# Dilated attention: first group's logits in two column tiles of 384 keys, value products cut to the rows a key block reaches

## The reference, cut to what matters

```python
off = np.arange(3 * blk)[None, :] - blk - np.arange(blk)[:, None]
band = np.abs(off) <= half            # half = window // (2 * dil) = 64
...
logits = einsum(q, k) * hd ** -0.5 + bias
logits = where(mask, logits, -1e30)
lse = logsumexp(logits);  p = exp(logits - lse);  o = einsum(p, v)
...
wgt = softmax(stack(lses));  o_b = sum(wgt[..., None] * stack(outs))
```

## Time and profile before

| | |
|---|---|
| time, median of 3 runs | 1826.12 us (1824.75 to 1828.1) |
| the profiled execution: time | 1826.74 us |
| its span, first to last instruction | 1825.0 us |
| PE busy | 1765.7 us, 97% |
| DVE, ACT, POOL busy | 801.9, 723.6, 604.0 us |
| mean granted clock of PE, as a share of 2.4 GHz | 0.988 |

### The profile page before, as it was taken

One profiled execution on the slowest core, in us unless ns is written; L12 is line 12 of the kernel. 1 busy time (PEld: TensorE's weight loads), 2 busy tenths in 40 slices (PEclk: granted clock), 3 DMA queues, 4 the chain that ended last, 5 costly groups with the idle time before them and its releaser, 6 DMA issues.

```text
span 1825.0 us, 25256 instructions
## 1 busy us (share of the span) xinstructions
PE 1765.7 (97%) x10862; PEld 1390.1 (76%) x10862; DVE 801.9 (44%) x1342; ACT 723.6 (40%) x1228; POOL 604.0 (33%) x182
## 2 busy tenths in 40 slices
PE   8999999999999999998999999989999999999997
PEld 5778899988888888877888888877684478776456
DVE  8756646623123121114670143145446654526653
ACT  5656665433233332233331222234426533345541
POOL 3534210333333434432454444424332114333112
PEclk9999999999999999998999999989999999999998
DMA  5121200326223323222222232213220012211001
GB/s 205 70 93 24 72 3 25 132 70 191 79 95 104 123 70 110 96 93 69 93 92 93 97 111 93 92 70 140 70 83 10 1 48 97 93 69 47 1 1 47
DMA packets 37504, 144.71 MB, mean 79 GB/s; under 512 B 3155, under 2 KB 15835, under 8 KB 23696
## 3 DMA queue, kind: packets, MB, share of 16 engines
q1 hardware_dynamic: 18944, 121.53, 18.8%
q10 hardware_dynamic: 18448, 21.57, 3.9%
HBM read 140.93 MB, written 5.30 MB: 80 GB/s over the span
## 4 chain that ended last, share of the span: by engine, by line
PE 87%; DVE 5%; ACT 4%; issue 1%; DMA 1%; ACTq 0%; POOL 0%; SPq 0%; POOLq 0%; DVEq 0%
PE bank L407 56%; PE bank L1145 6%; PE bank L613 5%; PE bank L418 4%; PE bank L2196 3%; PE bank L2220 3%; PE bank L2203 2%; DVE WK L978 1%; PE bank L1653 1%; PE bank L1629 1%; PE bank L2149 1%; ACT WK L2330 1%; ACT w_part L365 1%; PE bank L2228 1%; DMA WK<-wgate 1%
## 5 line engine op out<-in xcount | busy, mean ns | idle before, releaser
L407 PE MATMUL bank<-x_part,w_part 128*128 128x512 f32 x3216 | 746.8, 392 | 1.5 <-ACT WK L2309 0.8
L407 PEld LDWEIGHTS bank<-x_part,w_part 128*128 128x128 f32 x3216 | 601.0, 188 | 135.4 <-issue 10.7
L2660 POOL TENSOR_TENSOR w_part<-RAW,w_part 128x2048 fp32r<-128x2048 f32 (+1 forms) x90 | 404.2, 4493 | 678.4 <-ACT w_part L365 678.4
L365 ACT ACTIVATE w_part<-RAW 128x2048 fp32r<-128x2048 f32 (+1 forms) x90 | 165.8, 1842 | 175.5 <-PE bank L407 138.0
L2660 POOL TENSOR_TENSOR w_part<-WK,w_part 128x2048 fp32r<-128x2048 f32 (+1 forms) x30 | 123.7, 4124 | 246.9 <-ACT w_part L365 246.9
L407 PE MATMUL bank<-f_part,w_part 128*128 128x512 f32 x768 | 174.4, 389 | 0.0
L407 PEld LDWEIGHTS bank<-f_part,w_part 128*128 128x128 f32 x768 | 144.1, 188 | 29.9
L1145 PE MATMUL bank<-WK 64*64 64x64 f32 (+1 forms) x1456 | 103.4, 249 | 4.8 <-ACT WK L1311 2.5
L1145 PEld LDWEIGHTS bank<-WK 64*64 64x64 f32 (+1 forms) x1456 | 99.0, 163 | 7.3 <-ACT WK L1311 2.6
L978 DVE SCALAR_TENSOR_TENSOR WK<-bank,COL,WK 128x510 f32<-128x510 f32 (+1 forms) x96 | 71.7, 749 | 48.6 <-ACT WK L920 45.9
L2677 POOL TENSOR_TENSOR WK<-BASE,WK 128x1024 f32<-128x1024 f32 x16 | 30.4, 1898 | 167.5 <-DVE WK L2503 167.5
(11 more groups left out here) (286 smaller groups left out, 2236.1 us busy)
## 6 DMA issues: line engine op xcount, KB each, us to landing
RAW<-wts SPq DMA_DIRECT2D x83, 1024.0 KB, 4.8
WK<-wts SPq DMA_DIRECT2D x23, 1024.0 KB, 4.8
WK<-scratch ACTq DMA_DIRECT2D x16, 256.0 KB, 2.7
WK<-decay_rows ACTq DMA_DIRECT2D x14, 256.0 KB, 6.6
RAW<-wts SPq DMA_DIRECT2D x7, 512.0 KB, 3.5
WK<-wts SPq DMA_DIRECT2D x7, 512.0 KB, 3.4
scratch<-bias_rows ACTq DMA_DIRECT2D x4, 768.0 KB, 8.8
WK<-xT SPq DMA_DIRECT2D x4, 512.0 KB, 7.3
```

Source lines behind the costliest of these rows:

```text
L365: act.eng.activation(high_part(i), raw_part(i), ACT.Copy).then_inc(*act.did(("hi", i)))
L407: mm = pe.eng.matmul(b[:, :], W[w][:, k, c:c + P], src[x][k], start=start and k == 0 and n == 0, stop=stop and k == kn - 1 and n == 2)
L2660: eng.tensor_tensor(low_part(i), raw_part(i), high_part(i).bitcast(F32), ALU.subtract).then_inc(w_split, 1)
```

## The change

In group 0 the 128 queries of residue r are the tokens 4 l + r. The first 64 of them lie in tokens 0 to 255, the last 64 in tokens 256 to 511. With a reach of 64 keys the first half needs only keys 0 to 319 and the second half keys 192 to 511. The changed kernel gives each half 384 keys: 0 to 383 and 128 to 511. The halves are two products with 64 stationary columns each, written to PSUM partitions 0 to 63 and 64 to 127. A row of logits then has 384 + 256 elements in place of 512 + 256.

There are five transposes instead of six. The value product of group 0 becomes six products, three key blocks for each half, each of them only over the queries that the block reaches: widths 48, 48, 16 and 16, 48, 48. The two products of groups 1 and 2 come first, since they write all 128 columns. The bias tile of group 0 comes in two DMAs instead of one.

```diff
+        NEAR = 3 * P
-        LG = wk(31488, 2, 768)      (PT, BI alike)
+        LG = wk(31488, 2, NEAR + 2 * P)
+        REACH = ((0, 48), (16, 64), (48, 64)), ((64, 80), (64, 112), (80, P))
...
-                E.matmul(b[:, :], QB[:, 0, r * P:(r + 1) * P], KB[:, 0, :], start=True, stop=True).then_inc(...)
+                for a in range(2):
+                    mm = E.matmul(b[64 * a:64 * a + 64, 0:NEAR], QB[:, 0, r * P + 64 * a:r * P + 64 * a + 64],
+                                  KB[:, 0, a * P:a * P + NEAR], start=True, stop=True)
+                mm.then_inc(*pe.did(("pe", ("la", n))))
...
-                for k in range(4):
+                for k in range(3):
                     mm = E.transpose(a[:, k * P:(k + 1) * P], LG[:, n % 2, k * P:(k + 1) * P], ident)
...
-                for k in range(6):
-                    v = VB[:, k, 0:P] if k < 4 else VB[:, r, (k - 3) * P:(k - 2) * P]
-                    mm = E.matmul(o[:, 0:P], v, PT[:, n % 2, k * P:(k + 1) * P], start=k == 0, stop=k == 5)
+                for g in (1, 2):
+                    E.matmul(o[:, 0:P], VB[:, r, g * P:(g + 1) * P], PT[:, n % 2, NEAR + (g - 1) * P:NEAR + g * P], start=g == 1, stop=False)
+                for a in range(2):
+                    for k, (lo, hi) in enumerate(REACH[a]):
+                        mm = E.matmul(o[:, lo:hi], VB[:, k + a, 0:P], PT[:, n % 2, k * P + lo:k * P + hi], start=False,
+                                      stop=a == 1 and k == 2)
...
-                A.activation(PT[:, n % 2, 0:512], ps(("ta", n))[:, :], ACT.Copy)...
+                A.activation(PT[:, n % 2, 0:NEAR], ps(("ta", n))[:, 0:NEAR], ACT.Copy)...
...
-                A.dma_start(BI[:, n % 2, 0:512], a).then_inc(bias_in[n % 2], 16)
+                for h in range(2):
+                    a = bass.AP(..., offset=base + 511 - r + h * (64 * (1536 - DIL) + P), ap=[[1536 - DIL, 64], [1, NEAR]])
+                    A.dma_start(BI[64 * h:64 * h + 64, n % 2, 0:NEAR], a).then_inc(bias_in[n % 2], 16)
...
-                V.scalar_tensor_tensor(out=LG[:, n % 2, 0:512], in0=ps(("la", n))[:, :], ..., in1=BI[:, n % 2, 0:512], ...)
+                V.scalar_tensor_tensor(out=LG[:, n % 2, 0:NEAR], in0=ps(("la", n))[:, 0:NEAR], ..., in1=BI[:, n % 2, 0:NEAR], ...)
```

More of the change, by code:

```diff
@@ L1602, in build @@
         VB = wk(29952, TT, 3 * P)
-        LG = wk(31488, 2, 768)
-        PT = wk(33024, 2, 768)
-        BI = wk(34560, 2, 768)
+        NEAR = 3 * P
+        LG = wk(31488, 2, NEAR + 2 * P)
+        PT = wk(33024, 2, NEAR + 2 * P)
+        BI = wk(34560, 2, NEAR + 2 * P)
+        REACH = ((0, 48), (16, 64), (48, 64)), ((64, 80), (64, 112), (80, P))
         BR = wk(12288, 1536)
@@ L1628, in logits @@
                 b = job(("la", n))
-                E.matmul(b[:, :], QB[:, 0, r * P:(r + 1) * P], KB[:, 0, :], start=True, stop=True).then_inc(*pe.did(("pe", ("la", n))))
+                for a in range(2):
+                    mm = E.matmul(b[64 * a:64 * a + 64, 0:NEAR], QB[:, 0, r * P + 64 * a:r * P + 64 * a + 64], KB[:, 0, a * P:a * P + NEAR],
+                                  start=True, stop=True)
+                mm.then_inc(*pe.did(("pe", ("la", n))))
                 b = job(("lb", n))
@@ L1642, in turn @@
                 for k in range(2):
-                    mm = E.transpose(b[:, k * P:(k + 1) * P], LG[:, n % 2, (4 + k) * P:(5 + k) * P], ident)
+                    mm = E.transpose(b[:, k * P:(k + 1) * P], LG[:, n % 2, (3 + k) * P:(4 + k) * P], ident)
                 mm.then_inc(*pe.did(("pe", ("tb", n))))
@@ L1650, in av @@
                 o = job(("ob", n))
-                for k in range(6):
-                    v = VB[:, k, 0:P] if k < 4 else VB[:, r, (k - 3) * P:(k - 2) * P]
-                    mm = E.matmul(o[:, 0:P], v, PT[:, n % 2, k * P:(k + 1) * P], start=k == 0, stop=k == 5)
+                for g in (1, 2):
+                    E.matmul(o[:, 0:P], VB[:, r, g * P:(g + 1) * P], PT[:, n % 2, NEAR + (g - 1) * P:NEAR + g * P], start=g == 1, stop=False)
+                for a in range(2):
+                    for k, (lo, hi) in enumerate(REACH[a]):
+                        mm = E.matmul(o[:, lo:hi], VB[:, k + a, 0:P], PT[:, n % 2, k * P + lo:k * P + hi], start=False, stop=a == 1 and k == 2)
                 mm.then_inc(*pe.did(("pe", ("ob", n))))
@@ L1723, in moves @@
                     act.wait_ge(*at(("pe", ("ob", n - 2))))
-                A.activation(PT[:, n % 2, 0:512], ps(("ta", n))[:, :], ACT.Copy).then_inc(*act.did(("pta", n), free=("ta", n)))
+                A.activation(PT[:, n % 2, 0:NEAR], ps(("ta", n))[:, 0:NEAR], ACT.Copy).then_inc(*act.did(("pta", n), free=("ta", n)))
                 act.wait_ge(*at(("pe", ("tb", n))))
-                A.activation(PT[:, n % 2, 512:768], ps(("tb", n))[:, 0:256], ACT.Copy).then_inc(*act.did(("ptb", n), free=("tb", n)))
+                A.activation(PT[:, n % 2, NEAR:NEAR + 256], ps(("tb", n))[:, 0:256], ACT.Copy).then_inc(*act.did(("ptb", n), free=("tb", n)))
             def bias_row(j):
@@ L1748, in bias_tiles @@
                 base = hh * P * 1536
-                a = bass.AP(tensor=scratch.tensor, offset=base + 511 - r, ap=[[1536 - DIL, P], [1, 512]])
-                A.dma_start(BI[:, n % 2, 0:512], a).then_inc(bias_in[n % 2], 16)
+                for h in range(2):
+                    a = bass.AP(tensor=scratch.tensor, offset=base + 511 - r + h * (64 * (1536 - DIL) + P), ap=[[1536 - DIL, 64], [1, NEAR]])
+                    A.dma_start(BI[64 * h:64 * h + 64, n % 2, 0:NEAR], a).then_inc(bias_in[n % 2], 16)
                 b = bass.AP(tensor=scratch.tensor, offset=base + 1024 + 127, ap=[[1535, P], [256, 2], [1, P]])
-                A.dma_start(BI[:, n % 2, 512:768].rearrange("p (g c) -> p g c", g=2), b).then_inc(bias_in[n % 2], 16)
-                table[("bi", n)] = (bias_in[n % 2], 32 * (n // 2 + 1))
+                A.dma_start(BI[:, n % 2, NEAR:NEAR + 256].rearrange("p (g c) -> p g c", g=2), b).then_inc(bias_in[n % 2], 16)
+                table[("bi", n)] = (bias_in[n % 2], 48 * (n // 2 + 1))
             for hh in range(4):
@@ L1819, in logits @@
                 dve.wait_ge(*at(("pe", ("la", n))))
-                V.scalar_tensor_tensor(out=LG[:, n % 2, 0:512], in0=ps(("la", n))[:, :], scalar=float(P) ** -0.5, in1=BI[:, n % 2, 0:512],
+                V.scalar_tensor_tensor(out=LG[:, n % 2, 0:NEAR], in0=ps(("la", n))[:, 0:NEAR], scalar=float(P) ** -0.5, in1=BI[:, n % 2, 0:NEAR],
                                        op0=ALU.mult, op1=ALU.add).then_inc(*dve.did(free=("la", n)))
                 dve.wait_ge(*at(("pe", ("lb", n))))
-                V.scalar_tensor_tensor(out=LG[:, n % 2, 512:768], in0=ps(("lb", n))[:, 0:256], scalar=float(P) ** -0.5, in1=BI[:, n % 2, 512:768],
+                V.scalar_tensor_tensor(out=LG[:, n % 2, NEAR:NEAR + 256], in0=ps(("lb", n))[:, 0:256], scalar=float(P) ** -0.5,
+                                       in1=BI[:, n % 2, NEAR:NEAR + 256],
                                        op0=ALU.mult, op1=ALU.add).then_inc(*dve.did(("lg", n), free=("lb", n)))
```

## The result

The changed kernel takes 1831.43 us (median of 8 runs, 1828.87 to 1834.96) against 1824.91 us for the kernel before in its 8 runs (1822.2 to 1828.1). The ratio is 1.0039, with a 95% interval of 1.003 to 1.0047: 7.1 us slower by the ratio. The forecast was 7.2 us slower, 1833.3 us, in a range of 1829.5 to 1838. The absolute time is 1.9 us under the forecast, and 1.2 of these come from the base: the kernel before ran at 1824.91 in these runs and not at 1826.12.

A forecast was written before the change was run, and what follows sets the result against it. The prediction took PE to bound the kernel (97% busy). Value products +1.79, logits +0.34, transposes -0.22 and the wait -0.10 made +1.81 per head, +7.2 us over four heads: 1833.3 us, range 1829.5 to 1838.

The forecast's parts named there:

- Value products: In av, eight products instead of six: four more records at 0.112 us, +0.45 us for each n, +1.79 per head.
- Logits: Group 0's la in two column tiles: +0.13 us for n, n+1 and n+3, -0.05 for n+2, +0.34 per head.
- a trip: PE going from whole array into column tiles and back: 0.30 us beside the work, 0.34 around la.
- Transposes: One fewer for each n, 0.11 us; counts only for n+2 and n+3, -0.22 per head.
- the wait for ACT: PE waits before logits(n+2) for ACT's copy of turned probabilities; smaller copy gives -0.10 per head, PE's wait 0.12 longer.
- Nothing taken back after the stage: After the changed stage PE still sets the pace, 97% busy, so the +7.2 us stays.
- The DMA issues on ACT's queue: One more bias-tile issue for each n, 0.33 us, 16 in all; costs nothing, with 4.8 us of cover.
- Cheap narrow products: Rival in av: width counts, not the stationary load; gain 8.3 us there, 1817.9 us in all; chance 0.05.
- tiles that don't overlap: Rival in la: the two column tiles run one after the other, 10.3 us more, 1843.6 us; chance 0.04.
- a hidden switch: In la, the tile-shape switch costs nothing: logits give 3.5 us back instead of costing 1.4; within the 0.06 rival.
- the swallowed part: Rival: logits cost ahead of the wait for ACT vanishes, or the tile switch is hidden; 1828.4 us; chance 0.06.
- The granted clock: Rival: narrow products in paired av bring half clock for 3.3 us, 6.6 us in all, 1839.9 us; chance 0.07.

The follow-up runs named there:

- one_tile: Changed kernel with one 384-column logits product on the whole array instead of two column tiles, leaving out some needed keys: 1826.5 us, ratio 1.0011 to the kernel before.
- six_products: Changed kernel with six value products instead of eight, ACT's copy spreading the three turned blocks over four key blocks: 1822.79 us, ratio 0.9993 to the kernel before.
- paired_tiles: Kernel with tiles and six value products, reordered so the tiled logits of n and n+1 precede those of groups 1 and 2: 1821.5 us, ratio 0.9979 to before.
- reach_alone: Kernel before with only group 0's four value products narrowed to 48, 64, 64 and 48 columns, still six products: 1825.03 us, ratio 1.0001.
- eight_products: Kernel before with group 0's first and last value products split into two of 64 columns, eight products, same columns in all: 1831.48 us, ratio 1.0036.
- full_halves: Changed kernel with group 0's six value products each over all 64 queries of their half: 1831.6 us, ratio 1.0036 to the kernel before.

## Why the prediction was right, point by point

- **PE sets the pace, and its records are to be counted by the distance of starts.** Shown: the stage grew by 6.97 us, what follows it by nothing, and what DVE and ACT save (4 and 2 us of busy time in the stage) is nowhere in the time.
- **Value products, +1.79 per head.** Shown, by count alone (+1.84 per head with nothing else changed), by width alone (+0.06) and in the chain: two `av` went from 2.68 to 3.50 us there, 0.41 each; from the start of line 1657 to that of the projection behind it, 512.79 to 516.28, it is 3.49 against 2.60, 0.445 each, as predicted from the earlier trace rows.
- **Logits, +0.34 per head.** Shown by one_tile (1.18 of trips forecast, 1.20 measured) and by six_products (+0.05 for everything but the value products, +0.02 forecast). The price of 0.30 us for a trip was read from other operands, and it held: paired_tiles saved 0.34 for each trip left out. That the tiles start together shows in the trace too: in the window 510.01 to 510.02 two of the four records of `la` have started.
- **Transposes, only half of them counting, and the wait for ACT 0.10 shorter and 0.12 longer for PE.** Shown by the two kernels with a sixth transpose, the copy of 0.38 instead of 0.49 us, and the wait of 0.46 against 0.35 us in the second and third head.
- **Nothing taken back after the stage.** Shown by the windows. The stage grew by 6.97 us and not by 4 x 1.84 = 7.36, because in the profiled execution of before the first head took 64.59 us, 0.30 more than the others (its wait at line 1629 was 0.65 us, theirs 0.35), and after it took 66.13 like the rest. In the last head two things nearly cancel. After, its wait was 0.83 us, 0.37 more than in the others: ACT's rounding had first waited 0.25 us for the weights (why these came late is open). Before, it took 2.91 us from the start of the last pair of `av` to the projection behind it (657.79 to 660.70), 0.31 more than in the second head. What is left is about 0.15 us; the step into tiles ahead of the first `la`, some 0.1, lies outside the window, which would account for most of it.
- **The DMA issues on ACT's queue were mis-sized.** I put one more issue at 0.33 us. The two issues of 64 partitions take 0.55 us each (median) and the third went from 0.45 to 0.60, so the three take 1.70 us for each n instead of 0.78: 0.92 more, not 0.33. It stayed covered, as the list of waits shows no wait of PE for anything behind them; the 4.8 us of cover was much larger than either number.
- **The rivals.** Cheap narrow products are refuted by reach_alone and eight_products; tiles that don't overlap, a hidden switch and the swallowed part by one_tile. The granted clock was 1.00 in the stage, so the pairs of `av` did not bring it down; it was 1.00 there too in the profiled executions of eight_products and full_halves, with as many records in `av`. Nor did the clock fall behind the narrow products of the earlier trace rows each time. The same two windows in the profiled execution of the changed kernel, where nothing of that stage was changed:

```profile
63.80:66.60 2.80, 2.80 (x26) 2.77 (x24) 2.69 (x5) 1.89 (x2) 1.35 (x1) 1.00 0.43 126
66.90:70.20 3.30, 3.30 (x19) 2.14 (x12) 1.08 (x2) 2.32 (x5) 2.93 (x1) 1.00 0.43 176
```

What can't be settled with these runs is below the 0.1% or so that a comparison resolves: six_products is 0.05 us per head slower in the profile and 0.07% faster by its device time, with an interval that holds both.

## What to carry to other kernels

Before cutting a product to the elements that matter, ask what sets the distance of its records: here a float32 product with a 128x128 stationary operand is two records of 0.112 us each, at 16 columns as at 128, so below 128 columns only fewer products help, and a cut that adds products loses. A layout made for one product (halves with keys of their own) is paid for by the next one that reads it; here one access pattern in a copy that had to run anyway gave the shared operand back. Tiled products belong side by side in the order, since each trip from the whole array into column tiles and back cost about 0.3 us in both places where it was measured, with two products inside or with four.

## What the hardware showed that I had not expected

- A bias tile in two DMAs of 64 partitions takes longer to issue than one of 128: 0.55 us each against 0.33, and the unchanged DMA behind them rose from 0.45 to 0.60 us. The profile of the changed kernel, ACT's queue (durations in ns as least, median and greatest, then first and last start):

```profile
L1758 ACTq DMA_DIRECT2D WK<-scratch x32: 451/550/662, 427.1 to 630.9; - x32
...
L1760 ACTq DMA_DIRECT2D WK<-scratch x16: 602/602/609, 428.3 to 631.6; - x16
```

- An unchanged part of the program, the 427 to 430 us ahead of the stage, differed by 3.1 us between two executions, with a mean granted clock of 0.99 against 1.00. Before, the clock was granted at half speed, the 1.2 GHz level, in three stretches there, the one of the earlier trace rows and these two:

```profile
189.80:193.20 3.40, 3.40 (x66) 3.40 (x68) 1.27 (x3) 1.69 (x6) 2.50 (x2) 0.50 1.02 236
230.70:234.10 3.40, 3.40 (x38) 3.28 (x35) 0.42 (x1) 0.69 (x3) 0.00 (x0) 0.50 0.02 5
```

After, in one alone:

```profile
177.30:180.70 3.40, 3.36 (x16) 3.36 (x17) 3.40 (x8) 3.33 (x13) 2.81 (x4) 0.51 0.02 5
```

Two such stretches fewer, each 3.4 us at half speed, are 3.4 us by an estimate from these rows, about the 3.1 us. These 3.1 us are nearly half of the effect studied, and a single pair of spans would have given 3.8 us instead of 7.
